# First attention of a two-block transformer kernel: separate PSUM banks for scores and turned probabilities, a pipeline three steps deep, and gate products in single-tile pieces

## The chip, the cores and the metric

The kernel runs on one NeuronCore of a Trainium2 chip, as one launch with every input and output in device memory. The metric is the device time of the launch in microseconds (us). PE is TensorE (its matmuls; its weight loads are shown apart as PEld), DVE is VectorE, ACT is ScalarE, POOL is GpSimd, SP is SyncE.

## What is computed

A sequence of 256 tokens of width 1024 in float32 goes through two blocks. The second has two layers, which the change leaves alone. The first, cut to what matters here:

```
h = rmsnorm(x)
qa, ka, va, qb, kb, vb, ga, gb = split(h @ w_in)            # 5120 columns
qa, ka, qb, kb = per-head rmsnorm, then rotary on 16 of 64 columns
oa = dilated_attention(qa, ka, va)       # 12 heads in 3 groups of strides 1, 4, 16; 4 head slots,
                                         # the 3 groups joined by their log denominators
ob = sliding_window_attention(qb, kb, vb, window 128, sinks)  # 8 query heads, 2 key heads
mix = sigmoid(ga) * (oa @ w_branch_a) + sigmoid(gb) * (ob @ w_branch_b)
x = x + mix @ w_out
x = x + square(relu(rmsnorm(x) @ w_up)) @ w_down
```

## The kernel before

Every product with a weight matrix is made to nearly float32 precision from three passes: the weight is split into a high and a low part (`whi`, `wlo`), the activation likewise (`xt_hi`, `xt_lo`), and `tile_mm` (L1299) issues high by high, high by low and low by high for one block of 128 input rows, one tile of 128 tokens and 512 columns. Weights come in units of 1 MB, numbered in the order of use; two units make a strip of 512 columns of `w_in`. SP issues their loads in that order into a ring of five buffers (`load`, L302), each load waiting until PE has used the unit five places earlier (`used`). ACT makes the high part (`split_hi`, L406), DVE the low part (`split_lo`, L411).

Each engine has its own program, written out by hand, and runs it in order; semaphores tie them together. In the first block PE multiplies strips 0 to 5 (queries, keys, values) and strip 6 (the first gates), and then comes the stage that the change is about: the attention, with the last three strips of gates (units 14 to 19) laid between its pieces. The attention has 16 units: 0 to 7 are the dilated one (4 head slots by 2 token tiles; each takes the three groups together), 8 to 15 the window one (4 head pairs by 2 tiles). PE, ACT and DVE each run a loop over steps, and in step i:

- PE issues `scores(i)` (L1407, queries by keys into two PSUM banks), `turn_probs(i-1)` (L1415, transposes of the exponentials, into the banks from which unit i-1's scores have been read), `outputs(i-2)` (L1432, probabilities by values), and then the step's share of gate blocks (`STEP_BLOCKS`; a block is both token tiles for one k, six matmuls of 512 columns, `strip_block`).
- DVE runs `maxima(i)` (L846 or L855: scale, mask, row maximum, result to `ebuf1`; then the negated maximum, L850 or L858), `reciprocals(i-1)`, `read_out(i-2)` (L879), and in the steps of `STEP_SPLITS` a `split_lo`.
- ACT runs `exps(i)` (L565 or L570, and L575 for the sinks), `read_pt(i-1)` (L584, turned probabilities to `ptb1`), and in the steps of `STEP_SPLITS` the `split_hi` of the same unit.

Two sets of two banks take turns (`set_of`, L553): set u % 2 holds unit u's scores and then its turned probabilities. So `scores(u)` waits until ACT has copied unit u-2's turned probabilities out:

```
def scores(pe, u):
    if u >= 2:
        pe.wait_ge(pt_out, u - 1)
```

Banks 0 and 1 take the gate strips, banks 6 and 7 the outputs by turns. Before the steps, 12 tiles of queries and keys are transposed (`qk_pe`, L1386) in six events through banks 4 to 7 and copied by ACT (`read_qk`, L549); the last five tiles are turned in one go between steps 7 and 8. After the last step DVE drains and signals (`xt_src`), PE transposes all six tiles of the attention's results (L1329), ACT and DVE split them, and PE multiplies them with the branch weights: unit 20 (branch a) into banks 0 to 3, units 21 and 22 (branch b) into banks 4 to 7. DVE multiplies both with the gates, and the transposes of that mix (201.57 us in the profile) begin the product with `w_out`.

## Time and profile before

| | us |
|---|---|
| three runs | 1404.22, 1406.83, 1409.38 (median 1406.83) |
| the profiled execution | 1404.03 |
| its span, first to last instruction | 1402.4 |
| PE busy in it | 1346.8 (96%) |
| DVE busy | 829.3 (59%) |
| ACT busy | 619.4 (44%) |
| mean granted TensorE clock | 0.995 |

The span is read from the profiled execution, whose own time is 1.6 us above it. An engine's busy time counts its instructions, not its waits. A row of the timeline gives an instruction's start and length; matmuls overlap, so their pace is the distance between starts, not the length. A remark in brackets is the time that the engine was idle before the instruction, and who released it.

### The profile page before, as it was taken

To read this page: it belongs to the slowest core of one execution; us is meant where nothing else is said; L and a number is where in the kernel's file an instruction comes from. 1 tells how busy PE (TensorE), PEld (TensorE's weight loads), DVE (VectorE), ACT (ScalarE), POOL (GpSimd) and SP (SyncE) were. 2 spreads that over 40 slices of the span, in tenths; PEclk is the share of its full clock that TensorE was granted. 3 is DMA by queue.
4 is the path that set the end of the run, shared out by engine and by line. 5 is a ranking of instruction groups with operands and counts; after the bars stand their busy time and mean duration, and the time that the engine had idled before them with its cause. 6 is when DMAs were issued, how large, how long until landed. Compare 5 with 4: busy or idle time off the path is not lost.

```text
span 1402.4 us, 15837 instructions
## 1 busy us (share of the span) xinstructions
PE 1346.8 (96%) x6430; PEld 1091.8 (78%) x6430; DVE 829.3 (59%) x1128; ACT 619.4 (44%) x841; POOL 73.8 (5%) x132
## 2 busy tenths in 40 slices
PE   6998899999999999999999999999999999999997
PEld 5876677888887888886678888888888866788886
DVE  5674465645455544588785554664455877755445
ACT  4644534535235334435634433354434366353341
POOL 3321000000000000000110000000000002000000
PEclk9999999999999999999999999999999999999999
DMA  7651144655556555544266565565565441666550
GB/s 263 195 173 60 61 162 154 210 182 180 199 169 208 193 189 182 187 171 121 61 204 216 184 191 195 180 210 180 188 195 188 150 121 61 232 198 195 185 180 30
DMA packets 149336, 238.55 MB, mean 170 GB/s; under 512 B 5472, under 2 KB 97648, under 8 KB 149264
## 3 DMA queue, kind: packets, MB, share of 16 engines
q1 hardware_dynamic: 148880, 237.00, 51.8%
q8 instruction: 51, 0.84, 0.2%
q0 software_dynamic: 384, 0.54, 0.2%
q14 instruction: 21, 0.17, 0.0%
HBM read 236.47 MB, written 1.05 MB: 169 GB/s over the span
## 4 chain that ended last, share of the span: by engine, by line
PE 71%; issue 17%; DVE 4%; ACT 3%; DVEq 2%; POOL 2%; POOLq 1%; DMA 1%; SPq 0%; ACTq 0%
PE ps L1302 22%; PE ps L1304 21%; PE ps L1303 21%; PE ps L1555 2%; DVE stats L1068 1%; ACT whi L406 1%; PE ps L1348 1%; PE ps L1341 1%; PE ps L1342 1%; POOLq L425 1%; POOL lrs L431 1%; PE ps L1407 1%; POOL drs L426 1%; DVE wlo L411 1%; DVEq L1067 1%
## 5 line engine op out<-in xcount | busy, mean ns | idle before, releaser
L411 DVE TENSOR_TENSOR wlo<-raw,whi 128x2048 fp32r<-128x2048 f32 x217 | 491.3, 2289 | 154.0 <-ACT whi L406 154.0
L1302 PE MATMUL ps<-whi,xt_hi 128*128 128x512 f32 (+1 forms) x1064 | 424.4, 399 | 3.2 <-DVE wlo L411 2.6
L1304 PE MATMUL ps<-whi,xt_lo 128*128 128x512 f32 (+1 forms) x1064 | 412.8, 388 | 0.0
L406 ACT ACTIVATE whi<-raw 128x2048 fp32r<-128x2048 f32 x217 | 407.9, 1915 | 10.6 <-DMA raw<-in_w_up_dram 5.8
L1303 PE MATMUL ps<-wlo,xt_hi 128*128 128x512 f32 (+1 forms) x1064 | 411.8, 387 | 0.0
L1302 PEld LDWEIGHTS ps<-whi,xt_hi 128*128 128x128 f32 x1064 | 200.3, 188 | 52.1 <-issue 12.2
L1304 PEld LDWEIGHTS ps<-whi,xt_lo 128*128 128x128 f32 x1064 | 200.3, 188 | 41.9
L1303 PEld LDWEIGHTS ps<-wlo,xt_hi 128*128 128x128 f32 x1064 | 200.6, 189 | 36.2
L1302 PE MATMUL ps<-whi,ht_hi 128*128 128x512 f32 x480 | 187.6, 391 | 0.0
L1303 PE MATMUL ps<-wlo,ht_hi 128*128 128x512 f32 x480 | 186.8, 389 | 0.0
L1304 PE MATMUL ps<-whi,ht_lo 128*128 128x512 f32 x480 | 186.8, 389 | 0.0
L689 ACT ACTIVATE ht_hi<-ps 128x256 fp32r<-128x256 f32 (+1 forms) x104 | 38.2, 415 | 327.3 <-PE ps L1555 327.1
L1028 DVE TENSOR_TENSOR ht_lo<-ps,ht_hi 128x256 fp32r<-128x256 f32 (+1 forms) x104 | 43.9, 461 | 223.4 <-ACT ht_hi L689 223.4
L683 ACT ACTIVATE hid_a<-ps 128x256 f32<-128x256 f32 (+1 forms) x104 | 38.0, 414 | 153.1 <-PE ps L1304 150.6
L1304 PEld LDWEIGHTS ps<-whi,ht_lo 128*128 128x128 f32 x480 | 90.1, 188 | 18.8
L1302 PEld LDWEIGHTS ps<-whi,ht_hi 128*128 128x128 f32 x480 | 90.2, 188 | 18.5
L1303 PEld LDWEIGHTS ps<-wlo,ht_hi 128*128 128x128 f32 x480 | 90.1, 188 | 18.4
L510 ACT ACTIVATE xt_hi<-ps 128x512 fp32r<-128x512 f32 (+1 forms) x40 | 22.9, 587 | 118.5 <-PE ps L1329 118.5
L1021 DVE TENSOR_TENSOR hid_b<-hid_a,ps 128x256 f32<-128x256 f32 x88 | 33.4, 417 | 60.5 <-ACT hid_a L683 60.5
L1341 PE MATMUL ps<-whi,xt_hi 128*128 128x512 f32 x144 | 60.3, 419 | 4.3 <-DVE wlo L411 4.3
L431 POOL TENSOR_TENSOR lrs<-lrs,half 128x1 f32<-128x1 f32 x12 | 13.4, 1115 | 955.3 <-DVE lrs L1074 955.3
L1342 PE MATMUL ps<-wlo,xt_hi 128*128 128x512 f32 x144 | 58.5, 406 | 0.0
(178 smaller groups left out, 1042.6 us busy)
## 6 DMA issues: line engine op xcount, KB each, us to landing
raw<-in_ffn_w_in_dram SPq DMA_DIRECT2D x176, 512.0 KB
raw<-in_ffn_w_out_dram SPq DMA_DIRECT2D x44, 1024.0 KB
raw<-in_w_in_dram SPq DMA_DIRECT2D x38, 1024.0 KB
raw<-in_w_up_dram SPq DMA_DIRECT2D x16, 1024.0 KB
raw<-in_w_down_dram SPq DMA_DIRECT2D x16, 1024.0 KB
raw<-in_w_out_dram SPq DMA_DIRECT2D x8, 1024.0 KB
ln_g<-in_ln_g_dram SPq DMA_DIRECT2D x8, 512.0 KB, 6.8
raw<-in_w_out_dram SPq DMA_DIRECT2D x8, 512.0 KB
```

The lines of the kernel that those rows point to most:

```text
L406: act.activation(whi[j][:, :], raw[j][:, :], ACT.Copy).then_inc(hi_done, 1)
L411: dve.tensor_tensor(wlo[j][:, :], raw[j][:, :], whi[j][:, :].bitcast(F32), ALU.subtract).then_inc(lo_done, 1)
L683: act.activation(hid_a[:, t, 0:w], ps[:, 2 * par + t, 0:w], ACT.Silu if ffn else ACT.Relu).then_inc(hid_act, 1)
L689: act.activation(ht_hi[par][:, 0:k, t * P:(t + 1) * P], ps[:, 2 * par + t, 0:k * P].rearrange("p (k n) -> p k n", k=k), ACT.Copy).then_inc ...
L1021: dve.tensor_tensor(hid_b[:, t, 0:w], hid_a[:, t, 0:w], other, ALU.mult).then_inc(hid_ready, 1)
L1028: dve.tensor_tensor(ht_lo[par][:, 0:k, tok], ps[:, 2 * par + t, 0:k * P].rearrange("p (k n) -> p k n", k=k), ht_hi[par][:, 0:k, tok].bitca ...
L1302: pe.matmul(o, hi[:, k, tok], block_of(whi, u, b, width), start=start, stop=False)
L1303: pe.matmul(o, hi[:, k, tok], block_of(wlo, u, b, width), start=False, stop=False)
L1304: return pe.matmul(o, lo[:, k, tok], block_of(whi, u, b, width), start=False, stop=stop)
L1341: pe.matmul(o, xt_hi[:, k, tok], block_of(whi, u + k // 4, k % 4), start=k == 0, stop=False)
L1342: pe.matmul(o, xt_hi[:, k, tok], block_of(wlo, u + k // 4, k % 4), start=False, stop=False)
L1555: m = pe.transpose(ps[:, 2 * par + t, k * P:(k + 1) * P], hid_b[:, t, k * P:(k + 1) * P], ident[:, :])
```

## The change

- Scores always go to banks 2 and 3 (`scores1`), turned probabilities to banks 4 and 5 (`turned1`), outputs to bank 6, and the late transposes to bank 7. `scores(u)` now waits for the maxima of unit u-1 (`top_ready`), `turn_probs(u)` for the copy of unit u-1's turned probabilities (`pt_out`), `outputs(u)` for the reading of unit u-1's (`o_out`).
- The pipeline is one step deeper on PE: step i issues `scores(i)`, `turn_probs(i-2)`, `outputs(i-3)`, in 19 steps for 18. ACT's `read_pt` and DVE's `read_out` move along.
- A gate piece is one k of one token tile (three matmuls), all k of tile 0 first and then of tile 1; a third of a step's pieces stands between its scores and its transposes, the rest behind its outputs. Three pieces fill the turning of the first queries and keys. ACT reads each tile of a strip on its own. A unit is released (`used`) in the pass over tile 1.
- The splits have tables of their own for ACT (`STEP_HI`) and DVE (`STEP_LO`), DVE's one to two steps behind ACT's, and take in unit 23.
- The last queries and keys are turned one event a step (steps 5 to 7) through bank 7. The window units go through tile 0 first and then tile 1 (`unit1`). Branch a's input is turned after step 12 and its eight pieces lie in steps 16 to 18; branch b's is turned by token tile, after step 16 and inside its own products.

The diff, cut; a line of "..." marks what is left out:

```diff
-STEP_BLOCKS = (1, 1, 1, 1, 1, 1, 1, 1, 1, 1, 2, 2, 2, 2, 2, 2, 2, 0)
-STEP_SPLITS = {2: 16, 5: 17, 8: 18, 10: 19, 12: 20, 14: 21, 16: 22}
+
+
+QK1_FILL, GATE_FILL, BRANCH_FILL = 1, (3,) * 13 + (2,) * 3, {16: 3, 17: 3, 18: 2}
+STEP_HI = {0: 16, 2: 17, 5: 18, 7: 19, 9: 20, 11: 21, 13: 22, 16: 23}
+STEP_LO = {2: 16, 4: 17, 6: 18, 8: 19, 10: 20, 13: 21, 15: 22, 17: 23}
+SQUARES_3, SUMS_3, NORM_3, TURN_QB, TURN_OA, TURN_OB0 = 0, 1, 3, 5, 12, 16
...
+        oat_hi = sb("oat_hi", [P, TT, TOK], F32R, at=at_att + 56 * KB)
+        oat_lo = sb("oat_lo", [P, TT, TOK], F32R, at=at_att + 58 * KB)
...
+        def read_gate_tile(act, s, t):
+            c = (s - S1_GATES) * BW
+            if t == 0:
+                act.wait_ge(gate_tile, s - S1_SOLID + 1)
+            else:
+                act.wait_ge(used, 2 * s + 2)
+            act.activation(gates[:, t, c:c + BW], ps[:, t, :], ACT.Tanh, scale=0.5).then_inc(proj_out, 1)
...
+        def qk_bank(e):
+            return 4 + e % 4 if e < 6 else 7
...
-        def set_of(u):
-            b = 2 + 2 * (u % 2)
-            return ps[:, b:b + 2, :].rearrange("p b n -> p (b n)")
+        scores1 = ps[:, 2:4, :].rearrange("p b n -> p (b n)")
+        turned1 = ps[:, 4:6, :].rearrange("p b n -> p (b n)")
+
+        def unit1(u):
+
+
+            return (u // TT, u % TT) if u < HALF else ((u - HALF) % 4, (u - HALF) // 4)
...
-            for i in range(UNITS + 2):
-                if i in reads:
-                    read_gate(act, reads[i])
-                if i == 3:
+            for i in range(UNITS + 3):
+                for strip_tile in reads.get(i, ()):
+                    read_gate_tile(act, *strip_tile)
+                if i == SQUARES_3:
                     head_square(act, 3)
-                if i == UNITS // 2:
-                    read_qk(act, range(6, QK1_BANKS), 6, 2)
                 if i < UNITS:
                     exps(act, i)
-                if 1 <= i <= UNITS:
-                    read_pt(act, i - 1)
-                if i in STEP_SPLITS:
-                    split_hi(act, STEP_SPLITS[i])
-            xt_act(act, 1, 6)
-            split_hi(act, U_WOUT1)
+                if 0 <= i - 2 < UNITS:
+                    read_pt(act, i - 2)
+                if TURN_QB <= i < TURN_QB + 3:
+                    read_qk(act, (6 + i - TURN_QB,))
+                if i == TURN_OA:
+                    branch_a_act(act)
+                if i == TURN_OB0:
+                    branch_b_act(act, 0)
+                if i in STEP_HI:
+                    split_hi(act, STEP_HI[i])
+            branch_b_act(act, 1)
...
-            i, e, s = u % 4, ebuf1[u % 3], set_of(u)
+            i, e, s = u % 4, ebuf1[u % 3], scores1
...
-            for i in range(UNITS + 2):
+            for i in range(UNITS + 3):
                 if i < UNITS:
                     maxima(dve, i)
                 if 1 <= i <= UNITS:
                     reciprocals(dve, i - 1)
-                if i >= 2:
-                    if i == UNITS + 1:
-                        dve.drain()
-                    read_out(dve, i - 2)
-                if i == 3:
+                if i >= 3:
+                    read_out(dve, i - 3)
+                if i == SUMS_3:
                     sum_squares(dve, 3)
-                if i == 5:
+                if i == NORM_3:
                     norm_heads(dve, 3)
-                if i in STEP_SPLITS:
-                    split_lo(dve, STEP_SPLITS[i])
+                if i == TURN_OA + 1:
+                    branch_a_dve(dve)
+                if i == TURN_OB0 + 1:
+                    branch_b_dve(dve, 0)
+                if i in STEP_LO:
+                    split_lo(dve, STEP_LO[i])
             dve.drain().then_inc(xt_src, 4)
-            xt_dve(dve, 1, 6)
-
             dve.wait_ge(gate_half, S1 - S1_GATES)
             dve.wait_ge(used, U_BRANCH + 1)
             for t in range(TT):
...
         def scores(pe, u):
-            if u >= 2:
-                pe.wait_ge(pt_out, u - 1)
-            s, qt = set_of(u), u % TT
+            if u in (0, HALF):
+                pe.wait_ge(qk_out, 6 if u == 0 else QK1_BANKS)
+            if u >= 1:
+                pe.wait_ge(top_ready, u)
+            s, (h, qt) = scores1, unit1(u)
...
         def turn_probs(pe, u):
             pe.wait_ge(e_ready, u + 1)
-            s = set_of(u)
+            if u >= 1:
+                pe.wait_ge(pt_out, u)
             for j in range(width_of(u) // P):
-                m = pe.transpose(s[:, j * P:(j + 1) * P], ebuf1[u % 3][:, j * P:(j + 1) * P], ident[:, :])
+                m = pe.transpose(turned1[:, j * P:(j + 1) * P], ebuf1[u % 3][:, j * P:(j + 1) * P], ident[:, :])
             m.then_inc(pt_ready, 1)
 
         def outputs(pe, u):
             pe.wait_ge(pt_out, u + 1)
-            if u >= 2:
-                pe.wait_ge(o_out, u - 1)
-            o, pt, nk = ps[:, 6 + u % 2, :], ptb1[u % 2], u % TT + 1
+            if u >= 1:
+                pe.wait_ge(o_out, u)
+            o, pt, (h, qt) = ps[:, 6, :], ptb1[u % 2], unit1(u)
...
+        def gate_piece(pe, p):
+
+            s, t, k = S1_SOLID + p // (2 * KD), p // KD % 2, p % KD
+            if k == 0:
+                pe.wait_ge(proj_out, 2 * s - 1 + t)
+            if t == 0 and k % 4 == 0:
+                pe.wait_ge(lo_done, 2 * s + k // 4 + 1)
+            m = tile_mm(pe, xt_hi, xt_lo, k, 2 * s + k // 4, k % 4, t, t, k == 0, k == KD - 1)
+            if t == 1 and k % 4 == 3:
+                m.then_inc(used, 1)
+            if t == 0 and k == KD - 1:
+                m.then_inc(gate_tile, 1)
+
+        def branch_a_piece(pe, p):
+
+            t, h, k = p // 4, p // 2 % 2, p % 2
+            if p == 0:
+                pe.wait_ge(proj_out, 2 * S1)
+                pe.wait_ge(xt_lo_done, 5)
+                pe.wait_ge(lo_done, U_BRANCH + 1)
+            if p == 4:
+                pe.wait_ge(top_ready, UNITS)
+            m = tile_mm(pe, oat_hi, oat_lo, k, U_BRANCH, 2 * k + h, t, 2 * t + h, k == 0, k == 1)
+            if p == 7:
+                m.then_inc(used, 1)
+
+        def turn_branch_a(pe):
+            pe.wait_ge(o_out, HALF)
+            pe.wait_ge(qk_out, QK1_BANKS)
+            for k in range(2):
+                for t in range(TT):
+                    m = pe.transpose(ps[:, 7, (2 * k + t) * P:(2 * k + t + 1) * P], proj1[:, t, k * P:(k + 1) * P], ident[:, :])
+            m.then_inc(xt_tr, 1)
+
+        def turn_branch_b(pe, t):
+            pe.wait_ge(o_out, HALF + 4 * (t + 1))
+            pe.wait_ge(xt_lo_done, 5 + t)
+            for k in range(4):
+                m = pe.transpose(ps[:, 7, k * P:(k + 1) * P], proj1[:, t, OA_W + k * P:OA_W + (k + 1) * P], ident[:, :])
+            m.then_inc(xt_tr, 1 + t)
...
-            qk_pe(pe, range(6), 4, 4)
-            blocks = blocks_of_steps()
+            p = 0
+            for e in range(6):
+                qk_pe(pe, e)
+                if e >= 3:
+                    for _ in range(QK1_FILL):
+                        gate_piece(pe, p)
+                        p += 1
             pe.wait_ge(proj_out, 2 * S1_GATES)
-            for i in range(UNITS + 2):
-                if i == 0:
-                    pe.wait_ge(qk_out, 6)
-                if i == UNITS // 2:
-                    pe.wait_ge(roped, 4)
-                    pe.wait_ge(o_out, i - 2)
-                    qk_pe(pe, range(6, QK1_BANKS), 6, 2)
-                    pe.wait_ge(qk_out, QK1_BANKS)
+            for i in range(UNITS + 3):
+                n_fill = GATE_FILL[i] if i < UNITS else BRANCH_FILL[i]
+                piece = gate_piece if i < UNITS else branch_a_piece
+                if i == UNITS:
+                    p = 0
                 if i < UNITS:
                     scores(pe, i)
-                if 1 <= i <= UNITS:
-                    turn_probs(pe, i - 1)
-                if i >= 2:
-                    outputs(pe, i - 2)
-                for b in blocks[i]:
-                    s = S1_SOLID + b // KD
-                    if b % KD == 0:
-                        pe.wait_ge(proj_out, 2 * s)
-                    strip_block(pe, 2 * s, b % KD, pair(0))
+                for _ in range(n_fill // 2):
+                    piece(pe, p)
+                    p += 1
+                if 0 <= i - 2 < UNITS:
+                    turn_probs(pe, i - 2)
+                if i >= 3:
+                    outputs(pe, i - 3)
+                for _ in range(n_fill - n_fill // 2):
+                    piece(pe, p)
+                    p += 1
+                if TURN_QB <= i < TURN_QB + 3:
+                    qk_pe(pe, 6 + i - TURN_QB)
+                if i == TURN_OA:
+                    turn_branch_a(pe)
+                if i == TURN_OB0:
+                    turn_branch_b(pe, 0)
 
             for t in range(TT):
-                for b in range(2):
-                    xt_half_pe(pe, 1, t, b, proj1, 6)
-            pe.wait_ge(proj_out, 2 * S1)
-            pe.wait_ge(lo_done, U_BRANCH + 1)
-            for t in range(TT):
-                for h in range(2):
-                    pe.wait_ge(xt_lo_done, 4 + 2 * t + h + 1)
-                    for k in range(2):
-                        m = tile_mm(pe, xt_hi, xt_lo, k, U_BRANCH, 2 * k + h, t, 2 * t + h, k == 0, k == 1)
-            m.then_inc(used, 1)
-            for t in range(TT):
+                pe.wait_ge(xt_lo_done, 6 + 2 * t)
                 for j in range(2):
                     u = U_BRANCH + 1 + j
                     if t == 0:
                         pe.wait_ge(lo_done, u + 1)
+                    if t == 0 and j == 1:
+                        turn_branch_b(pe, 1)
```

How the order of the instructions moves on PE, at two places. First, step 10 of the attention before (the kernel's buffer numbers are part of the names; `qkt` are turned queries and keys, `ebuf` exponentials, `ptb` turned probabilities, `proj` the projections):

```order
L1407 MATMUL ps<-qkt_82 128x128 [waits pt_out]
L1407 MATMUL ps<-qkt_82 128x128
L1415 MATMUL ps<-ident,ebuf_0_83 128x128 [waits e_ready]
L1415 MATMUL ps<-ident,ebuf_0_83 128x128 x3
L1432 MATMUL ps<-proj_81,ptb_0_86 128x64 [waits o_out,pt_out]
L1432 MATMUL ps<-proj_81,ptb_0_86 128x64
L1302 MATMUL ps<-whi_64,xt_hi 128x512
L1303 MATMUL ps<-wlo_57,xt_hi 128x512
L1304 MATMUL ps<-whi_64,xt_lo 128x512
```

and the same step of the change:

```order
L1453 MATMUL ps<-qkt_82 128x128 [waits top_ready]
L1453 MATMUL ps<-qkt_82 128x128
L1346 MATMUL ps<-whi_66,xt_hi 128x512
L1347 MATMUL ps<-wlo_59,xt_hi 128x512
L1348 MATMUL ps<-whi_66,xt_lo 128x512
L1462 MATMUL ps<-ident,ebuf_2_85 128x128 [waits pt_out,e_ready]
L1462 MATMUL ps<-ident,ebuf_2_85 128x128
L1479 MATMUL ps<-proj_81,ptb_1_87 128x64 [waits o_out,pt_out]
L1479 MATMUL ps<-proj_81,ptb_1_87 128x64 x5
```

The wait of the scores has changed its semaphore, and a piece of three matmuls has come between scores and transposes. Second, the end of the stage before, behind the last gate block:

```order
L1432 MATMUL ps<-proj_81,ptb_1_87 128x64 [waits o_out,pt_out]
L1432 MATMUL ps<-proj_81,ptb_1_87 128x64 x3
L1329 MATMUL ps<-ident,proj_81 128x128 [waits xt_src]
L1329 MATMUL ps<-ident,proj_81 128x128 x3
L1329 MATMUL ps<-ident,proj_81 128x128 [waits xt_src]
L1329 MATMUL ps<-ident,proj_81 128x128
L1329 MATMUL ps<-ident,proj_81 128x128 [waits xt_src]
L1329 MATMUL ps<-ident,proj_81 128x128 x3
L1329 MATMUL ps<-ident,proj_81 128x128 [waits xt_src]
L1329 MATMUL ps<-ident,proj_81 128x128
L1302 MATMUL ps<-whi_63,xt_hi 128x512 [waits xt_lo_done,lo_done,proj_out]
```

and of the change, from the end of step 16 into step 17:

```order
L1520 MATMUL ps<-ident,proj_81 128x128 [waits xt_lo_done,o_out]
L1520 MATMUL ps<-ident,proj_81 128x128 x3
L1346 MATMUL ps<-whi_63,oat_hi 128x512
L1347 MATMUL ps<-wlo_56,oat_hi 128x512
L1348 MATMUL ps<-whi_63,oat_lo 128x512
L1462 MATMUL ps<-ident,ebuf_0_83 128x128 [waits pt_out,e_ready]
L1462 MATMUL ps<-ident,ebuf_0_83 128x128 x3
L1479 MATMUL ps<-proj_81,ptb_0_86 128x64 [waits o_out,pt_out]
L1479 MATMUL ps<-proj_81,ptb_0_86 128x64 x3
L1346 MATMUL ps<-whi_63,oat_hi 128x512 [waits top_ready]
```

Branch a's products (those on `oat`) now lie among the last transposes and outputs, and the results are turned in groups of four transposes in place of twelve in a row.

## Rows read from the trace of the kernel before

**Rows 1.** The page: span; busy time of each engine

```profile
span 1402.4 us, 15837 instructions
PE 1346.8 (96%) x6430; PEld 1091.8 (78%) x6430; DVE 829.3 (59%) x1128; ACT 619.4 (44%) x841; POOL 73.8 (5%) x132
```

**Rows 2.** By stretch: PE, PEld, DVE, ACT, POOL busy; TensorE clock, DMA share, GB/s

```profile
94.70:201.60 106.90, 91.14 (x512) 72.07 (x510) 54.89 (x158) 52.30 (x111) 9.87 (x8) 0.98 0.23 79
170.00:175.00 5.00, 5.00 (x19) 3.81 (x17) 1.94 (x11) 3.53 (x8) 0.00 (x0) 0.66 0.01 3
175.00:180.00 5.00, 5.00 (x31) 4.07 (x31) 3.42 (x13) 1.74 (x7) 0.00 (x0) 1.00 0.67 210
201.60:231.00 29.40, 25.93 (x123) 21.32 (x123) 18.85 (x16) 10.75 (x10) 0.75 (x2) 1.00 0.66 232
625.00:690.00 65.00, 63.39 (x360) 43.26 (x359) 50.42 (x151) 39.56 (x108) 1.06 (x2) 1.00 0.42 114
```

**Rows 3.** Waits of PE, 85 to 200 us: total us, times, longest

```profile
PE ps L1407 <- ACT ptb L584: 11.0, 6, 3.1
PE ps L1407 <- ACT qkt L549: 1.9, 2, 1.4
PE ps L1329 <- DVEq L1193: 1.4, 1, 1.4
PE ps L1386 <- ACT qkt L549: 0.8, 1, 0.8
PE ps L1302 <- DVE xt_lo L834: 0.6, 1, 0.6
```

**Rows 4.** Timeline, 141 to 149 us: start, us, engine, line, [idle before <-releaser]

```profile
141.09 1.90 ACT L406 ACTIVATE whi<-raw 128x2048 fp32r<-128x2048 f32 x1
...
143.01 2.29 DVE L411 TENSOR_TENSOR wlo<-raw,whi 128x2048 fp32r<-128x2048 f32 x1 [3.01 <-ACT whi L406]
...
146.14 0.16 DVE L858 SCALAR_TENSOR_TENSOR ntop<-top,nsink 128x2 f32<-128x2 f32 x1
...
146.33 0.51 ACT L570 ACTIVATE ebuf<-ebuf,ntop 128x256 f32<-128x256 f32 x1 [3.35 <-DVE ntop L858]
...
147.70 0.36 ACT L584 ACTIVATE ptb<-ps 128x256 f32<-128x256 f32 x1
...
148.12 0.49 PE L1407 MATMUL ps<-qkt 64*128 64x128 f32 x4 [3.07 <-ACT ptb L584]
...
149.40 0.48 PE L1302 MATMUL ps<-whi,xt_hi 128*128 128x512 f32 x1
```

**Rows 5.** Timeline of PE in the first layer's attention, same columns

```profile
647.13 0.40 PE L1304 MATMUL ps<-whi,xt_lo 128*128 128x512 f32 x1
647.46 0.70 PE L1469 MATMUL ps<-qkt 64*128 64x256 f32 x4
648.09 0.50 PE L1302 MATMUL ps<-whi,xt_hi 128*128 128x512 f32 x1
648.43 0.39 PE L1303 MATMUL ps<-wlo,xt_hi 128*128 128x512 f32 x1
648.66 0.39 PE L1304 MATMUL ps<-whi,xt_lo 128*128 128x512 f32 x1
```

**Rows 6.** Timeline of PE where the clock was low, same columns

```profile
171.32 0.63 PE L1304 MATMUL ps<-whi,xt_lo 128*128 128x512 f32 x1
171.75 0.63 PE L1302 MATMUL ps<-whi,xt_hi 128*128 128x512 f32 x1
```

**Rows 7.** Timeline of SyncE, the issues of the loads for `w_out`

```profile
175.14 26.96 SPq L306 DMA_DIRECT2D raw<-in_w_out_dram  x4
```

**Rows 8.** Groups by form, 94.7 to 201.6: count, busy us, mean ns, idle

```profile
L526 ACT ACTIVATE gates<-ps 128x512 f32<-128x512 f32 x8 | 4.3, 590 | 6.5 <-PE ps L1304 6.5
...
L846 DVE CUSTOM_DVE_ANT_0 ebuf<-ps,mask 128x768 f32<-128x768 f32 x4 | 3.8, 956 | 6.7 <-PE ps L1407 6.7
...
L565 ACT ACTIVATE ebuf<-ebuf,ntop 128x768 f32<-128x768 f32 x4 | 3.7, 936 | 10.5 <-DVE ntop L850 10.5
```

More of the change, by code:

```diff
@@ L511, in xt_act, with branch_a_act, branch_b_act @@
                                    ACT.Copy).then_inc(xt_hi_done, 1)
+        def branch_a_act(act):
+            act.wait_ge(xt_tr, 5)
+            act.activation(oat_hi[:, :, :], ps[:, 7, :].rearrange("p (k n) -> p k n", k=2), ACT.Copy).then_inc(xt_hi_done, 1)
+        def branch_b_act(act, t):
+            act.wait_ge(xt_tr, 6 + 2 * t)
+            act.activation(xt_hi[:, 2:6, t * P:(t + 1) * P], ps[:, 7, :].rearrange("p (k n) -> p k n", k=4),
+                           ACT.Copy).then_inc(xt_hi_done, 1 + t)
         def paired(ap, heads):
@@ L543, in read_gate, with read_qk @@
             read_strip(act, 2 * s + 2, [(0, BW, lambda t: gates[:, t, c:c + BW])], (0, 1), ACT.Tanh, 0.5)
-        def read_qk(act, events, bank0, banks):
+        def read_gate_tile(act, s, t):
[7 more added lines that the diff above has]
+            return 4 + e % 4 if e < 6 else 7
+        def read_qk(act, events):
             for e in events:
@@ L583, in read_pt @@
                 act.wait_ge(o_ready, u - 1)
-            act.activation(ptb1[u % 2][:, 0:w], set_of(u)[:, 0:w], ACT.Copy).then_inc(pt_out, 1)
+            act.activation(ptb1[u % 2][:, 0:w], turned1[:, 0:w], ACT.Copy).then_inc(pt_out, 1)
         def window_unit(f):
@@ L872, in read_out @@
             dve.wait_ge(o_ready, u + 1)
-            o, qt = ps[:, 6 + u % 2, :], u % TT
+            o, (h, qt) = ps[:, 6, :], unit1(u)
             if u < HALF:
-                cols = [u // TT * HD]
+                cols = [h * HD]
             else:
-                cols = [OA_W + (4 * r + (u - HALF) // TT) * HD for r in range(KV)]
+                cols = [OA_W + (4 * r + h) * HD for r in range(KV)]
             for r, c in enumerate(cols):
@@ L1377, in tiles_strip, with qk_pe @@
                     m.then_inc(y_done, 1)
-        def qk_pe(pe, events, bank0, banks):
-            for e in events:
-                if e >= banks:
-                    pe.wait_ge(qk_out, e - banks + 1)
-                for i in range(min(2, QK1_TILES - 2 * e)):
-                    for t in range(TT):
-                        m = pe.transpose(ps[:, bank0 + e % banks, (2 * i + t) * P:(2 * i + t + 1) * P],
-                                         qk_src1(2 * e + i, t), ident[:, :])
-                m.then_inc(qk_tr, 1)
+        def qk_pe(pe, e):
+            if e == 6:
+                pe.wait_ge(roped, 4)
+            before = e - 4 if e < 6 else e - 1
+            if before >= 0:
+                pe.wait_ge(qk_out, before + 1)
+            for i in range(min(2, QK1_TILES - 2 * e)):
+                for t in range(TT):
+                    m = pe.transpose(ps[:, qk_bank(e), (2 * i + t) * P:(2 * i + t + 1) * P],
+                                     qk_src1(2 * e + i, t), ident[:, :])
+            m.then_inc(qk_tr, 1)
         def qk_src1(tile, t):
@@ L1394, in scores @@
         def scores(pe, u):
-            if u >= 2:
-                pe.wait_ge(pt_out, u - 1)
-            s, qt = set_of(u), u % TT
+            if u in (0, HALF):
[3 more added lines that the diff above has]
+            s, (h, qt) = scores1, unit1(u)
             n = P * (qt + 1)
             if u < HALF:
-                h = u // TT
                 parts = [(h % 2, 2 * g + h // 2, 6 + 2 * g + h // 2) for g in range(DIL_G)]
             else:
-                parts = [(r, 12 + (u - HALF) // TT, 16) for r in range(KV)]
+                parts = [(r, 12 + h, 16) for r in range(KV)]
             for i, (r, qtile, ktile) in enumerate(parts):
@@ L1433, in outputs @@
             m.then_inc(o_ready, 1)
+        def gate_piece(pe, p):
[24 more added lines that the diff above has]
+            for k in range(2):
+                for t in range(TT):
+                    m = pe.transpose(ps[:, 7, (2 * k + t) * P:(2 * k + t + 1) * P], proj1[:, t, k * P:(k + 1) * P], ident[:, :])
[6 more added lines that the diff above has]
+            m.then_inc(xt_tr, 1 + t)
         def layer_turn_qk(pe, l, what, tile, tiles, col, heads):
```

43 lines of the change are left out of this document (26 added, 17 removed).

## The prediction

> **What bounds the kernel now.** I read the page first: PE is busy 1346.8 of 1402.4 us [rows 1], so only its 55.6 us of idle time and what its work costs can move the end. Busy time by stretch then shows where the idle time lies: in the stage that the change rewrites, from the first transposes of queries and keys (94.70 us) to the transposes of the mix (201.6), PE is busy 91.14 of 106.90 us [rows 2], so 15.8 us, over a quarter of all the idle time, lie here. DVE has 54.9 and ACT 52.3 us of work in it and the DMA engines are 0.23 busy [rows 2]: none of them is full. The waits of PE name the causes [rows 3]: 11.0 us in six waits of the scores for ACT's copy of turned probabilities (`ptb`), 1.9 and 0.8 for its copy of turned queries and keys, 1.4 for DVE's drain at the end, 0.6 for the split of the attention's result; 15.7 together, the idle time of the stage.
>
> The longest of them shows how the six come about [rows 4]. ACT splits a unit (141.09, 1.90 long). DVE, waiting since its last step, does the low part at 143.01 for 2.29. Behind it in DVE's queue stand the maxima, which end with the row at 146.14. Only then can ACT take the exponentials (146.33), and behind these in its queue stands the copy of the other unit's probabilities (147.70), for which the scores at 148.12 wait: 3.07 us idle. Two queues in series hold a copy that has long been possible.
>
> **What the change does to it, part by part.** *The scores' wait* becomes one for the maxima of the unit before. They ran, at their widest, 956 ns [rows 8], and PE now has a whole step of its own work between the scores and the next scores, so this wait should not show. The copy is waited for by `turn_probs` instead, one step later than its exponentials' unit. The chain that must fit is: maxima, exponentials, copy. From the end of the low part (143.01 + 2.29) to the scores it took 2.8 us [rows 4]. Against it PE has, from one unit's scores to the transposes of the next step, four pieces of three matmuls at 0.23 us each (distance of starts, [rows 5]), 2.8, plus the narrow work of a step, 1.28 in a window unit from 148.12 to 149.40 [rows 4], plus two changes of shape, 0.4 (below): 4.5. It fits by 1.7, but with a low part (2.29) in front it misses by 0.6. Since ACT's split now runs a step or more ahead, DVE no longer waits for it, and the low part often falls into DVE's own slack. The 11.0 go: **-11.0**.
>
> *The first transposes.* Three pieces (2.0 us of PE's work, which it had to do anyway) stand where PE waited 1.4 for ACT's six copies: -1.4. *The late transposes*, three events in a row with 0.8 and 0.5 of waiting, lie a step apart through a bank of their own: -1.3. Together **-2.7**. But the last event is still directly followed by `scores(8)`, which waits for its copy; the like wait was 0.5 (1.9 less 1.4, [rows 3]): **+0.5**. *The end*: no drain and no twelve transposes in a row, each group is split while PE has other pieces: -1.4 and -0.6, **-2.0**. What is late next there is the last gate strip: branch a's first piece writes bank 0 or 1 and waits for ACT's reading of the last tile, which PE has just finished: one read of 590 ns [rows 8] and two hand-offs, **+0.8**.
>
> *New waits around low parts.* Four of the eight low parts lie in steps of window units (8, 10, 13, 15), where a step is shortest; step 13 has also the split of branch a, and steps 13 to 15 have two pieces instead of three. At 0.6 each this bounds it at 2.4 from above; nothing, if the slack takes it, is the bound from below. I take **+1.4**, nearer to the first for step 13. Another row speaks to the sum of new waits: the first layer's attention, which has the same shape, left PE idle 1.6 us of 65 [rows 2], which over this stage would be 2.4; mine come to 0.5 + 0.8 + 1.4 = 2.7.
>
> *More changes of shape.* A run of wide matmuls is entered and left more often: by the two orders there are 18 runs in the stage before and 38 after, with the same 204 wide matmuls. In the first layer's attention the step from a wide matmul to narrow ones takes 0.33 us (647.13 to 647.46) and the first wide one behind narrow ones 0.34 (648.09 to 648.43), against 0.23 inside a run [rows 5]: 0.21 a run, 20 runs more, **+4.2**. This is the price of the edit and lies wholly on PE. Where PE would have waited anyway it costs nothing, so 3.0 is my lower bound.
>
> *The clock.* Between 170 and 175 us the granted clock was 0.66 in the mean [rows 2], so 0.68 of that time at the lower of its two levels (1.2 in place of 2.4 GHz): matmuls start 0.43 us apart there [rows 6] and not 0.23. 3.4 us at half pace cost 1.7. It happened in a stretch with waits of up to 3.1 us [rows 3]. If the waits go, so should this: **-1.7**. Bounds: nothing won, or twice as much, since a mean of 0.995 over the span says that there are more such drops, which could fall otherwise. The Trainium skill, "TensorE: Matmul & The Clock Gate", section "Part 1: The HAM clock gate (the "warmup" mystery)", says that idling lowers the clock and activity gives it back; the trace agrees (0.66 against 1.00 five us later). By the section "A second HAM failure mode: psum-queue depth-cycling" many small pauses alone can make the clock swing; by that rule the 20 more changes of shape could cost what the waits gave back. The first layer's attention, at 1.00 with as many changes, speaks against it [rows 2].
>
> *Costs of nothing.* Matmuls, transposes, exponentials, maxima, splits and loads stay the same in number. Single-tile reading of gates adds none. The loads: units are released in the pass over tile 1, a quarter of a strip later. A load of 1 MB at the 210 GB/s of 175 to 180 us [rows 2] takes 5 us, SP issues those of `w_out` from 175.14 on [rows 7], and the tables leave at least two and a half steps, some 8 us, between release and split. If that cover went, a split would wait for its load. Behind 201.6 us nothing changes: what PE waits for up to 231 us (3.5 us, [rows 2]) hangs on the product with `w_out`.
>
> **Sum.** -11.0 - 2.7 - 2.0 - 1.7 + 4.2 + 0.5 + 0.8 + 1.4 = -10.5 us, against the profiled execution's 1404.0: 1393.5. The median of the runs is 1406.8, 2.8 above that execution; on the same footing **1396.3 us** is what I expect of a median. The stage should last 96.4 us.
>
> **The rivals.**
>
> *A. The narrow steps run behind.* DVE and ACT lose their lead in the window units, and every one of these eight steps waits 0.6 to 1 us where I have 1.4 in all. For it: the chain with a low part misses by 0.6. Against: only every second step has a low part. 8 x 0.9 = 7.2, less the 1.4 counted: 5.8 later than forecast, 1402.1.
>
> *B. Buffers give nothing.* [...] As a mechanism of this kernel: separate banks only let PE run ahead until the next unit isn't split, the 15.7 us come back as waits for weights, the stage keeps its length, and the changes of shape hide in these waits: 1406.8. Against it: no wait of PE in this stage names a load or a low part [rows 3], and DMA is 0.23 busy.
>
> *C. Slower.* The single set of score banks makes a ring: scores(i), maxima(i), scores(i+1), in one queue with the low part. Should every maxima stand behind a full low part that itself starts only after `read_out`, which waits for PE's outputs of the same step, each of the eight split steps adds 2.3, 18.4 in all, in place of 11.0 + 1.4 counted: the sum is -10.5 - 1.4 + 18.4 = +6.5, so 1413.3. It decides from the point where new waits pass 2.7 + 10.5 = 13.2 us, or 0.8 in each step. Against it: DVE has 55 us of work for a stage of 96.
>
> *D. The change doesn't do what it says*: excluded by the order of instructions, which shows the new waits and pieces.
>
> **How the numbers follow.** What a measurement can tell from no change is about 0.3%, 4.2 us. The forecast (a gain of 7 to 14, 1393 to 1400) has 0.80, all of it faster. A has 0.11, mostly still faster. B has 0.05: the same. C has 0.04: slower. So 0.89 faster, 0.07 within, 0.04 slower. For the range: below, the clock's second drop (-1.7), changes of shape at 3.0 (-1.2) and new waits at 1.6 (-1.1) give 1392.3, and runs spread by 2.6 about their median: 1391. Above, it reaches A: 1402.5. That leaves out B, C and the edge of A.
>
> **What would show it.** Right: in the new profile the stage from the first transposes to those of the mix lasts 95 to 98 us; no scores wait for `ptb`; PE's waits there are below 4 us, the longest at branch a's first piece (for `gates`) and at `scores(8)` (for `qkt`), and some in steps 13 to 15 for `ptb` or maxima; the granted clock is 1.00 throughout it; starts at a change of shape stay at 0.33. Wrong: waits over 8 us in it, whatever they name (A or C), a wait for `wlo` (B), a clock below 1.00 in it, or changes of shape above 0.21 a run.

## The result, and the profile after

The changed kernel took 1389.16 us (median of 4 runs, 1386.91 to 1390.52), the kernel before 1408.11 beside it (4 runs, three of them those of its table): a ratio of 0.9871, 95% interval 0.9852 to 0.9891. It is faster, as forecast, but by 18.9 us where 10.5 were expected, and the time lies below the range (1391.0 to 1402.5). The profiled execution took 1386.91 and is the fastest of the four. The top of its page, then its waits of PE over the stage, then busy time by stretch, of the change and, in the last line, of the kernel before (columns as in [rows 1 to 3]):

```profile
span 1385.3 us, 15856 instructions
PE 1343.0 (97%) x6430; PEld 1088.7 (79%) x6430; DVE 828.8 (60%) x1127; ACT 619.5 (45%) x840; POOL 76.8 (6%) x132
```

```profile
PE ps L1346 <- ACT gates L565: 0.7, 1, 0.7
PE ps L1453 <- DVE ntop L901: 0.5, 1, 0.5
PE ps L1462 <- ACT ptb L613: 0.5, 1, 0.5
PE ps L1453 <- ACT qkt L574: 0.5, 1, 0.5
```

```profile
94.11:186.01 91.90, 89.69 (x511) 70.59 (x510) 54.69 (x157) 52.36 (x110) 12.84 (x8) 1.00 0.28 92
186.01:245.00 58.99, 55.53 (x265) 45.97 (x265) 42.70 (x45) 30.08 (x29) 1.50 (x4) 1.00 0.59 205
...
230.00:235.00 5.00, 4.11 (x17) 3.45 (x18) 3.40 (x5) 2.23 (x4) 0.19 (x1) 0.72 0.35 90
```

The span is 17.1 us shorter. 0.6 of that lies ahead of the stage (it begins at 94.11, not at 94.70), in a part that the change leaves alone; over all profiles the beginning lay between 93.7 and 95.1. The stage went from 106.9 to 91.9: **-15.0**, forecast -10.5. Behind it 1.5 more are gone: the profile before had a granted clock of 0.72 from 230 to 235 us, this one has 1.00 up to 245. That is a matter of the execution, not of the change alone: half of the runs of the change show a lower mean clock (end of the experiments). The 15.7 us of waits of [rows 3] have become 2.2, all four at places that the prediction had named, if not at their sizes, and PE's busy time in the stage fell from 91.14 us, with 3.4 of them at half clock [rows 2], to 89.69.

### The profile page after: what moved, and what is told of

It is laid out like the page before. It is cut to its first block, busy times and chain, and to the rows that moved or that the text cites. A ratio compares the mean times of both kernels' runs of the same rounds, so it can differ in the third digit from the quotient of the medians.

```text
span 1385.3 us, 15856 instructions
## 1 busy us (share of the span) xinstructions
PE 1343.0 (97%) x6430; PEld 1088.7 (79%) x6430; DVE 828.8 (60%) x1127; ACT 619.5 (45%) x840; POOL 76.8 (6%) x132
## 4 chain that ended last, share of the span: by engine, by line
PE 74%; issue 17%; DVE 4%; POOL 2%; ACT 1%; DVEq 1%; POOLq 1%; DMA 1%; SPq 0%; ACTq 0%
PE ps L1346 22%; PE ps L1348 22%; PE ps L1347 22%; PE ps L1643 2%; DVE stats L1111 1%; PE ps L1392 1%; PE ps L1453 1%; PE ps L1385 1%; PE ps L1386 1%; POOLq L432 1%; POOL lrs L438 1%; POOL drs L433 1%; PE ps L1479 1%; DVE wlo L418 1%; DVEq L1110 1%
## 5 line engine op out<-in xcount | busy, mean ns | idle before, releaser
L1348 PEld LDWEIGHTS ps<-whi,ht_lo 128*128 128x128 f32 x480 | 90.1, 188 | 18.9
L1347 PEld LDWEIGHTS ps<-wlo,ht_hi 128*128 128x128 f32 x480 | 90.2, 188 | 18.5
L514 ACT ACTIVATE xt_hi<-ps 128x512 fp32r<-128x512 f32 x36 | 21.3, 597 | 107.5 <-PE ps L1373 107.5
```

The lines of the kernel that those rows point to most:

```text
L1347: pe.matmul(o, hi[:, k, tok], block_of(wlo, u, b, width), start=False, stop=False)
L1348: return pe.matmul(o, lo[:, k, tok], block_of(whi, u, b, width), start=False, stop=stop)
```

## The experiments

Twelve kernels ran in three more sessions, one of them the change again. For each profile I took four numbers of the stage: its length, PE's waits in it, what a lower clock cost in it (time at 1.2 GHz times 0.20/0.43, the distances of starts of [rows 5, 6], from stretches of 5 us), and the rest. Each kernel has one profile. The column `runs` counts the runs of wide matmuls (512 columns) in the order of PE.

```
kernel                   stage  waits  clock  rest  runs | median us, ratio to before, 95%
before                   106.9   15.7    1.6  89.6   18  | 1405.6 to 1408.1 by session
change                    91.9    2.2    0    89.7   38  | 1389.16  0.9871 0.9852-0.9891
e1_pieces_together        91.9    2.8    0    89.1   24  | 1388.99  0.9866 0.9847-0.9886
e2_pieces_apart           92.0    2.5    0    89.5   49  | 1389.65  0.9871 0.9851-0.9891
e3_splits_coupled        102.0    7.1    4.7  90.2   38  | 1400.48  0.9949 0.9931-0.9967
e4_lead_alone            100.7    6.6    4.7  89.4   18  | 1396.67  0.9925 0.9908-0.9942
e5_two_deep               91.4    1.7    0    89.7       | 1388.22  0.9871 0.9856-0.9886
e6_end_in_sequence        95.0    3.6    1.6  89.8       | 1392.27  0.9901 0.9886-0.9915
e7_three_moves            91.7    2.2    0    89.5       | 1388.89  0.9876 0.9859-0.9893
e8_changed_again          91.9    2.2    0    89.7   38  | 1386.50  0.9865 0.9847-0.9883
e9_no_waits_three_deep    89.6    0.4    0    89.2       | 1386.21  0.9861 0.9846-0.9875
e10_no_waits_two_deep     89.6    0.4    0    89.2       | 1385.69  0.9857 0.9842-0.9872
e11_shared_banks_wait     93.5    3.8    0    89.7       | 1391.41  0.9899 0.9884-0.9913
e12_one_wait              94.7    4.9    0    89.8       | 1391.83  0.9902 0.9885-0.9920
```

The rest is 89.1 to 90.2 in all fourteen: but for these 1.1 us, waits and clock tell the kernels apart.

### What a run of wide matmuls costs

```diff
# e1_pieces_together, on the changed kernel
-                for _ in range(n_fill // 2):
+                first = 0 if i < UNITS else n_fill // 2
+                for _ in range(first):
...
# e2_pieces_apart, on the changed kernel: one piece between turn_probs and outputs
+                middle = 1 if 3 <= i < UNITS else 0
...
+                for _ in range(middle):
+                    piece(pe, p)
+                    p += 1
...
-                for _ in range(n_fill - n_fill // 2):
+                for _ in range(n_fill - first - middle):
```

> The changed kernel, but in steps 0 to 15 all pieces of the gate product stand behind the step's outputs and none between scores and transposes: 24 runs of wide matmuls in the stage in place of 38, all else in place. Forecast's price (0.21 a run, all on PE): the stage gets 14 x 0.21 = 2.9 us shorter, 91.9 to 89.0, less any new waits, and the whole 0.2% faster. Price by the starts in the two traces (0.10 to enter a run from narrow work, nothing to go from it to transposes, and transposes directly behind scores 0.06 slower than behind wide matmuls): 14 x 0.04 = 0.6 us shorter, 91.3, the same within what can be measured. Either way PE gets to the transposes one piece (0.7) earlier, so waits for ntop or ebuf beyond today's 2.2 us would show what the piece in front of them hides; I expect 0 to 2 us of them.

> The changed kernel, but in steps 3 to 12 the three pieces stand apart: one behind the scores, one between transposes and outputs, one behind the outputs; 48 runs of wide matmuls in place of 38. Forecast's price (0.21 a run): 10 x 0.21 = 2.1 us longer, stage 94.0. Price by the starts in the traces (0.10 to enter, going to outputs no more than the 0.23 that it is to transposes): 1.0 us longer, 92.9. New waits should not come: the outputs come later, and read_out and the maxima have slack.

With 24 runs the stage lasted as long as with 38 (0.6 less of work, 0.6 more of waits), and with 49 (one more than I had counted) 0.1 longer, with 0.3 more of waits and 0.2 less of the rest. Neither stage is where its text had put it (89.0 or 91.3, 94.0 or 92.9), but both are nearer to the lower price. In the second the wait for ntop, which should not have grown, went from 0.5 to 1.3, and that for gates from 0.7 to 0.2. The forecast's price would have made 25 x 0.21 = 5.3 us between the two; the rest differs by 0.4. The same step, with the same work (scores of 4 matmuls, 6 transposes, 6 narrow products, 9 wide matmuls), shows why. Timelines of PE ("..." marks rows left out), the changed kernel and then the one with pieces together:

```profile
140.37 0.49 PE L1453 MATMUL ps<-qkt 64*128 64x128 f32 x4
140.79 0.50 PE L1346 MATMUL ps<-whi,xt_hi 128*128 128x512 f32 x1
141.13 0.40 PE L1347 MATMUL ps<-wlo,xt_hi 128*128 128x512 f32 x1
141.37 0.40 PE L1348 MATMUL ps<-whi,xt_lo 128*128 128x512 f32 x1
141.60 0.82 PE L1462 MATMUL ps<-ident,ebuf 128*128 128x128 f32 x6
142.26 0.78 PE L1479 MATMUL ps<-proj,ptb 128*128 128x64 f32 x6
142.85 0.47 PE L1346 MATMUL ps<-whi,xt_hi 128*128 128x512 f32 x1
...
144.41 0.49 PE L1453 MATMUL ps<-qkt 64*128 64x128 f32 x4
```

```profile
140.45 0.49 PE L1453 MATMUL ps<-qkt 64*128 64x128 f32 x4
140.87 0.88 PE L1462 MATMUL ps<-ident,ebuf 128*128 128x128 f32 x6
141.58 0.78 PE L1479 MATMUL ps<-proj,ptb 128*128 128x64 f32 x6
142.17 0.48 PE L1346 MATMUL ps<-whi,xt_hi 128*128 128x512 f32 x1
...
144.43 0.49 PE L1453 MATMUL ps<-qkt 64*128 64x128 f32 x4
```

4.04 us against 3.98, and in the kernel with pieces apart 4.03 (141.38 to 145.41). Entering wide matmuls behind the scores costs 0.11 (140.79 to 141.13, against 0.23). But going from them to the transposes costs nothing (141.37 to 141.60), and the six transposes then take 0.66 and not 0.71 (140.87 to 141.58), since scores to transposes is a change of shape too; with wide matmuls on both sides, in the kernel with pieces apart, they took 0.57. So what it costs to enter a further run comes back, nearly, as a shorter narrow group beside it. Only from wide matmuls to scores does leaving cost 0.10, and that place exists in every order.

### ACT's lead

```diff
# e3_splits_coupled, on the changed kernel
-STEP_HI = {0: 16, 2: 17, 5: 18, 7: 19, 9: 20, 11: 21, 13: 22, 16: 23}
+STEP_HI = {2: 16, 4: 17, 6: 18, 8: 19, 10: 20, 13: 21, 15: 22, 17: 23}
# e4_lead_alone, on the kernel before
+STEP_HI = {i - 1: u for i, u in STEP_SPLITS.items()}
...
-                if i in STEP_SPLITS:
-                    split_hi(act, STEP_SPLITS[i])
+                if i in STEP_HI:
+                    split_hi(act, STEP_HI[i])
```

> The changed kernel, but ACT splits each unit in the same step as DVE makes its low part (2, 4, 6, 8, 10, 13, 15, 17), as before; separate banks, depth and end stay. If ACT's lead is a needed part: DVE waits up to 1.9 us for ACT in front of each low part, the maxima come later, and with the 0.6 by which the chain already misses, the four low parts in window steps cost some 1 to 2.5 us each, those in the other steps less: stage 96 to 99, waits of PE 6 to 9 us, for ntop and ptb. If separate banks and depth alone do it: stage 92 to 92.5 and waits as in the changed kernel.

> The kernel before, with only ACT's split of each unit one step ahead of DVE's low part. The banks, the order of PE and the end stay as before. If the coupling of the two queues is what made the six waits long: each loses the 1.9 us of ACT's split that stood in it, up to 6 x 1.6 = 9.6 of 11.0 us, stage 98 to 100. If the shared banks are the cause (ptb's copy stands behind the exponentials, and these behind maxima behind a low part of 2.29 us): 1 to 1.5 us are left in each wait, and the stage is 101 to 104 us.

Without the lead the change keeps 4.9 of its 15.0 us; the lead alone gives 6.2 to the kernel before, with its shared banks. The waits of PE in the two stages, first the change without the lead, then the kernel before with it:

```profile
PE ps L1453 <- DVE ntop L901: 3.3, 2, 2.8
PE ps L1453 <- ACT qkt L574: 2.6, 1, 2.6
```

```profile
PE ps L1408 <- ACT ptb L585: 3.3, 2, 2.5
PE ps L1408 <- ACT qkt L550: 1.9, 2, 1.4
```

The waits for `ptb` fell from 11.0 in six to 3.3 in two: 7.7 less, where the expectation of the lead gave up to 9.6 and that of the shared banks 2 to 5. So the coupling of the two queues made most of them, and the stage, 100.7, lies between the two expectations because of the clock. In the other run 2.6 of the waits were not for ntop or ptb, as expected, but for `qkt`: ACT's copy stood behind exponentials that came late, after a low part that had waited 4.03 us for ACT's split. Both profiles also hold what I had not priced for them: 4.7 us each lost to a lower clock, 3.1 more than in the kernel before. Of the coupled one, by stretch, the stage and behind its waits of 2.63 (until 138.56) and 2.79 (until 171.49):

```profile
94.50:196.47 101.97, 94.73 (x511) 74.26 (x510) 55.34 (x157) 52.70 (x110) 11.40 (x8) 0.95 0.26 83
139.00:146.00 7.00, 7.00 (x28) 5.70 (x28) 3.40 (x9) 3.42 (x8) 0.00 (x0) 0.55 0.44 152
174.00:178.00 4.00, 3.38 (x13) 2.59 (x12) 1.26 (x3) 3.76 (x8) 0.00 (x0) 0.60 0.00 0
```

PE is busy for all of the first stretch and for 3.4 of the 4 us of the second, at a mean granted clock of 0.55 and 0.60, so mostly at 1.2 GHz. That is why the stage came to 102.0, not the expected 96 to 99, with waits (7.1) inside the expected 6 to 9.

### Depth, banks, end

```diff
# e5_two_deep, on the changed kernel (ACT and DVE alike)
-                if 0 <= i - 2 < UNITS:
-                    turn_probs(pe, i - 2)
-                if i >= 3:
-                    outputs(pe, i - 3)
+                if 0 <= i - 1 < UNITS:
+                    turn_probs(pe, i - 1)
+                if 2 <= i < UNITS + 2:
+                    outputs(pe, i - 2)
# e11_shared_banks_wait: e5, and in scores
+            if u >= 2:
+                pe.wait_ge(pt_out, u - 1)
# e6_end_in_sequence, on the changed kernel, pieces of branch a behind the outputs
-... BRANCH_FILL = 1, (3,) * 13 + (2,) * 3, {16: 3, 17: 3, 18: 2}
+... BRANCH_FILL = 1, (3,) * 13 + (2,) * 3, {16: 0, 17: 0, 18: 8}
```

> The changed kernel with separate banks and ACT's lead kept, but two steps deep: transposes in the step after the scores, outputs in the step after that. Between a unit's scores and its transposes PE then has one step of about 3.8 us, against maxima and exponentials of 2.4 (head units) to 3.0 us (window units), plus ACT's split of 1.9 or DVE's low part of 2.29 in front in 16 of the steps. If the third step is a needed part: waits of the transposes for ebuf (ACT's exponentials) of 0.5 to 1 us in the window steps with a split, 4 to 8 us in all, stage 94 to 98 and perhaps a drop of the clock (3 to 5 us more, as in the two runs above). If depth gives nothing beyond the banks: stage 91.5 to 92.5.

> The changed kernel two steps deep, in which scores also wait for the copy of the unit two before, as if scores and turned probabilities still shared their banks. All else (ACT's lead, late and early transposes, the end) is as in the change. If separate banks are a needed part: behind a low part or a split, maxima, exponentials and copy take up to 5.5 us against a step of some 3.8, so 1 to 2 us in four to six steps: waits for ptb of 3 to 8 us, stage 94 to 99, perhaps with a drop of the clock. If ACT's lead had done it all: stage 91.4 to 92, as without this wait.

> The changed kernel, but all eight pieces of branch a stand behind the last outputs and none in steps 16 to 18. If beginning branch a early pays: PE then waits in steps 16 to 18 for copies and exponentials (0.6 for a copy, 1.9 for maxima and exponentials of the last unit) and for DVE's reading before the second group of branch b's transposes; 2 to 4 us more waits, stage 94 to 96. If the 0.7 for gates, which vanishes here, and the fewer changes outweigh it: stage 91 to 92.

The third step gives nothing: two deep, the stage is 0.5 us shorter, by the wait for ntop (and e9 and e10 below, which differ in depth alone, both have 89.6). My 4 to 8 us of waits for `ebuf` were wrong: no transposes waited for it. The wait that shared banks would bring costs 2.2 us (93.5 against 91.4). Its waits for `ptb`, four and none above 1.2, come to 2.5, under the 3 to 8 expected, and the stage is under the 94 to 99:

```profile
PE ps L1455 <- ACT ptb L613: 2.5, 4, 1.2
```

Once ACT runs ahead, the banks are the smaller part. Branch a at the end costs 3.1. The stage, 95.0, is the expected one, but in part by luck: the waits grew by 1.4 (3.6 against 2.2) where 2 to 4 were expected, and 1.6 of clock behind them, which I had not priced, made up the sum. The waits aren't for copies and exponentials either but for DVE's reading of the single output bank, 1.5 and 0.7 for the last units (the 0.7 for gates goes):

```profile
PE ps L1479 <- DVE proj L922: 2.1, 2, 1.5
```

### The four waits left, and one put in

Two of the four, for ntop and ptb, fall in step 15. The changed kernel around them:

```profile
158.71 0.68 DVE L862 TENSOR_TENSOR oat_lo<-ps,oat_hi 128x512 fp32r<-128x512 f32 x1
...
159.31 2.28 DVE L418 TENSOR_TENSOR wlo<-raw,whi 128x2048 fp32r<-128x2048 f32 x1
...
162.42 0.16 DVE L901 SCALAR_TENSOR_TENSOR ntop<-top,nsink 128x2 f32<-128x2 f32 x1
...
162.64 0.70 PE L1453 MATMUL ps<-qkt 64*128 64x256 f32 x4 [0.49 <-DVE ntop L901]
...
163.99 0.57 ACT L613 ACTIVATE ptb<-ps 128x512 f32<-128x512 f32 x1
...
164.71 0.63 PE L1462 MATMUL ps<-ident,ebuf 128*128 128x128 f32 x4 [0.47 <-ACT ptb L613]
...
166.61 2.28 DVE L418 TENSOR_TENSOR wlo<-raw,whi 128x2048 fp32r<-128x2048 f32 x1
```

In DVE's queue the maxima of step 14 stand behind branch a's split and the low part of step 13 (159.31); ACT's exponentials and its copy follow them. The low part of step 15 (166.61) comes after both waits.

```diff
# e7, e9 and e10, on the changed kernel (e10 two deep); the late transposes move up from behind the pieces
-                for _ in range(n_fill // 2):
+                first = n_fill // 2 if i != UNITS else 0
+                for _ in range(first):
...
                 if i >= 3:
                     outputs(pe, i - 3)
+                if TURN_QB <= i < TURN_QB + 3:
+                    qk_pe(pe, 6 + i - TURN_QB)
...
# e7: the low parts of units 21 to 23, and ACT's split of 23, a step earlier
-STEP_HI = {... 13: 22, 16: 23}
-STEP_LO = {... 10: 20, 13: 21, 15: 22, 17: 23}
+STEP_HI = {... 13: 22, 15: 23}
+STEP_LO = {... 10: 20, 12: 21, 14: 22, 16: 23}
# e9 and e10: no low part in steps 13 to 15; STEP_HI as in the change
+STEP_LO = {... 10: 20, 12: 21, 16: 22, 17: 23}
# e12_one_wait, on the changed kernel, behind the scores
+                if i == 9:
+                    pe.wait_ge(esink_ready, i + 1 - HALF)
```

> The changed kernel with three moves against its four waits (2.2 us): branch a's first piece behind the transposes and outputs of step 16 (0.7 for gates), the late transposes in front of the last pieces of their step (0.5 for qkt), and low parts of units 21, 22 and 23 a step earlier, so that none falls together with branch a's split in step 13 (0.5 for ntop and, in its wake, 0.5 for ptb). Waits in the stage 0.5 or less, stage 90.0, and the median 1.5 to 2.2 us below that of the changed kernel. Rival: the low part one step earlier now stands in step 14 in front of the first short steps and waits of 0.5 to 1 for ntop come back one step on: stage 91 to 92.

> The changed kernel once more. Its stage should last 91.9 us within 0.2. Its time hangs on whether the granted clock drops behind the wait of 3.5 us for the first normed tile some 29 us behind the stage: with the drop 1390 and a mean clock of 0.995, without it 1387 and 0.999. If the drop is the usual case, four of six runs or more lie at 1389 to 1391; if the first profile was the usual case, at 1387.

> The changed kernel with branch a's first piece behind transposes and outputs of step 16, the late transposes in front of the last pieces of their step, and low parts of units 21 and 22 in steps 12 and 16 (not 13 and 15); ACT's splits stay. If the four waits are DVE's and ACT's queues at these places: at most 0.5 us of the 2.2 is left, stage 89.7 to 90.3. If a low part in any late step costs its wait somewhere (as in the run with three moves, where 1.5 for ptb came in place of 1.0): stage 91 to 92.

> The same moves, two steps deep. The run two steps deep had the stage at 91.35 with 1.7 us of waits (qkt 0.5, gates 0.7, ptb 0.5). With qkt and gates gone: stage 90.0 to 90.5. If the third step is what covers a low part in step 12: waits of 1 us or more for ebuf, stage 91 to 92.

> The changed kernel with one wait put in: behind the scores of step 9 PE waits for that unit's exponentials, about 2.7 us in a stage that otherwise waits 0.7 at most at once. If a wait costs its idle time and no more: stage 91.9 + 2.7 = 94.6, less what it gives later waits. If a single wait of this size lowers the granted clock behind it, as behind the 2.5, 2.6 and 2.8 us of the earlier runs: 3 to 5 us more, stage 97 to 99. If it does so in some executions only: the runs fall in two groups, about 3 us apart.

The first attempt failed as its rival said, in another place: the low part in step 14 held the maxima back, one wait of 1.5 for `ptb` came in place of two of 0.5, and ACT's split of unit 23, a step earlier, stood in front of the reading of gates. With steps 13 to 15 free of low parts, and that split back in its place, one wait was left, in both e9 and e10:

```profile
PE ps L1462 <- ACT ptb L613: 0.4, 1, 0.4
```

The stage is 89.6 us, 2.3 shorter than the change's: 1.8 of it waits, 0.5 of it in the rest. All eight runs of the two lie at 1384.96 to 1386.34; the change's eight, of two other sessions, at 1386.29 to 1390.52. The intervals of the ratios overlap, so that these kernels are faster than the change rests on the stage more than on the medians.

The wait put in was 2.71 us long, and the stage 94.7 for 91.9: 2.8. Its clock stayed at 1.00 in the stage and behind the wait, and the four runs lie together, at 1391.6 to 1392.2: a wait of this size cost its idle time and no more. The clock fell only later, within the wait for `normed` (here 3.5, until 217.77) that stands in every profile some 30 us after the stage:

```profile
93.73:188.43 94.70, 89.79 (x512) 70.60 (x510) 55.52 (x157) 52.60 (x110) 12.86 (x8) 1.00 0.28 90
143.00:148.00 5.00, 4.80 (x28) 3.82 (x29) 0.85 (x6) 3.25 (x4) 0.00 (x0) 1.00 0.22 21
216.00:223.00 7.00, 5.23 (x17) 4.35 (x18) 3.39 (x5) 2.23 (x4) 0.89 (x3) 0.53 0.36 101
```

The changed kernel again gave 1386.29, 1386.47 and 1386.52 at mean clocks of 0.998 and 0.999, and 1390.03 at 0.995. With the first session's 1386.91 (0.999), 1388.26 (0.996), 1390.07 and 1390.52 (0.995), four of eight runs have no drop by their mean clock, three have all of it and one a part: neither of the two cases I had named is the usual one. Both profiled executions of the change had none in the stage or up to 245 us.

## Why the prediction was wrong in size

**Changes of shape, +4.2: this is the step that failed.** Waits and clock together: 15.7 + 1.6 - 2.2 = 15.1, and the stage lost 15.0, so twenty more runs cost about 0.1. The distances of [rows 5] were read rightly (0.33 and 0.34 are 0.33 and 0.34 here too), but compared with a run of wide matmuls inside, 0.23, as if a piece put between scores and transposes added two boundaries and took none away. It takes one away, and the transposes' side has no price. The lower bound of 3.0 rested on the same comparison, and with it the range's lower end, 1391 (where I also took off 1.3 for a spread of 2.6; with all of it, 1389.7, the end would still have been above the 1389.2 measured).

The median came 7.1 us under the 1396.3 forecast. 4.1 of it is this term, 0.5 the new waits, less 0.1 for the clock (1.6, not 1.7). 2.1 lie outside the stage, where I had put nothing: 0.6 ahead of it, and 1.5 behind it, where this execution has no drop of the clock. The last 0.5 is the step from execution to median. Of the signs named in advance the length of the stage, 95 to 98, failed with the term; the others came.

**Scores' wait, -11.0: right in sum, incomplete in cause.** No scores wait for `ptb` any more. I gave the lead one sentence and the separate banks the paragraph. By the runs the lead is the larger part (+10.1 without it, 4.7 of it clock; -6.2 by itself, which is 9.1 less of waits and 3.1 more of clock), the banks 2.2, the third step nothing. The parts don't add up, as I read it because one wait can have either cause.

**Transposes, -2.7, and the end, -2.0: right.** None of these waits is left. That beginning branch a early is worth it was shown for branch a alone; an order with twelve transposes in a row wasn't tried again.

**New waits, 2.7: measured 2.2.** `scores(8)` for `qkt` 0.5, as forecast; gates 0.7 for 0.8; ntop and ptb 0.5 each in place of 1.4, both in step 15, in the wake of the low part that step 13 ends with. That this low part is the cause is shown by the order of DVE's queue (above) and by the runs: with it in step 12, and none up to step 15, they were gone but for 0.4.

**Clock, -1.7: right in the stage,** 1.00 throughout. But the median of before lies higher than its profiled execution, and a lower clock goes with it: in the 22 executions of before in the three sessions a mean clock of 0.995 goes with 1403.6 to 1405.2 us and 0.991 with 1407.1 to 1408.5. The change's runs at 0.995 take 1390.0 to 1390.5, so 14 us less at the same mean clock; the other 4 to 5 of the 18.9 between medians go with fewer drops. I had carried the 2.8 us from execution to median over unchanged; it came out as 2.3, so this cost the forecast little. Where the other executions of before had their drops isn't known, as only one was profiled.

The rivals are out: A and C needed more and longer waits than 2.2 us in all, B a wait for a load or a low part, and none is there. The Trainium skill, "TensorE: Matmul & The Clock Gate", section "A second HAM failure mode: psum-queue depth-cycling", by which many small pauses alone can make the clock swing, is not borne out here: with 49 runs of wide matmuls the stage stayed at 1.00.

## What to carry to other kernels

Price an inserted piece by the whole step with and without it, both boundaries it makes less the one it takes away, not by the distance at its edges. When two engines serve a third through one split, let the first run a step ahead before buying buffers: a table of steps gave back more here than a pair of banks. Then look where several background jobs meet in one short step, and move one of them: three small moves brought the stage from 91.9 to 89.6 us.

## What the runs showed that I had not expected

A wait's price can be more than twice its length. Behind waits of 2.63, 2.79, 1.95 (before, until 169.25) and 1.48 + 0.66 in 3 us (e6) the clock was at its lower level for some 3 to 7 us, though PE was busy again; in e4 for 10 us from the end of a wait of 2.48. By the price used in the table 6.8 us at that level cost 3.2 and 10.2 us cost 4.7, an estimate. Behind single waits of 2.71 (e12) and 3.07 (before, until 148.12) it stayed at 1.00. The kernel before even has the same wait of 2.48 at the same scores, and no drop behind it. First before, then e4, the wait and the stretch behind it:

```profile
130.42 0.91 PE L1407 MATMUL ps<-qkt 64*128 64x256 f32 x3 [2.48 <-ACT ptb L584]
...
131.00:138.00 7.00, 5.74 (x40) 4.56 (x38) 1.48 (x5) 3.85 (x8) 1.05 (x1) 1.00 0.21 57
```

```profile
127.95 1.64 PE L1408 MATMUL ps<-qkt 64*128 64x256 f32 x3 [2.48 <-ACT ptb L585]
...
128.00:137.00 9.00, 9.00 (x29) 7.28 (x30) 1.47 (x5) 3.34 (x5) 0.00 (x0) 0.50 0.00 0
```

So the length alone doesn't decide, and what does stays open. The wait of 3.1 to 4.4 us for `normed` had a drop within or behind it in every profile but the two of the changed kernel, whose waits there were 3.5 and 3.4: also open.
